# Ring order of layer one, a silu behind evictions, and the entrances of block 2's projections in halves

## What is computed

```python
def _layer(x, ctx, mod_lat, mod_ctx, ...):
    sh, sc, gt = jnp.split(mod_lat, 3, axis=-1)
    xn = _rms_norm(x, g_norm) * (1 + sc[:, None]) + sh[:, None]
    (au, av, az, bq, bk, bv, bz, cq, ck, cv, co, cz, cg) = _split_proj(xn @ w_in)
    ...
    y_a = _gmlp_branch(au, av, az, w_s, b_s)      # ... * silu(az)
    x = x + gt[:, None] * (jnp.concatenate([y_a, y_b, y_c], axis=-1) @ w_out)
...
def second_block(x, c, w_ada, ...):
    for i in range(DEPTH):
        mod = (ada_in @ w_ada[i] + b_ada[i]).reshape(b, 6, d)
        ...
        hm = rmsnorm(x, norm_mix[i]) * (1 + sc_m) + sh_m
        if i % N_MIXERS == 0:
            y = dilated_mixer(hm, ...)            # proj = hm @ w_in, 9216 columns
        else:
            y = forgetting_mixer(hm, ...)         # proj = hm @ w_in, 3088 columns
        x = x + g_m * y
        hf = rmsnorm(x, norm_ffn[i]) * (1 + sc_f) + sh_f
        x = x + g_f * hierarchical_moe(hf, ...)
```

## Time and profile before

| | us |
|---|---|
| median of 3 runs | 1784.41 |
| lowest, highest | 1781.46, 1784.58 |
| the profiled execution | 1783.85 |
| its span, first to last instruction | 1782.0 |
| PE busy | 1588.5 (89%) |
| DVE busy | 1001.6 (56%) |
| ACT busy | 680.4 (38%) |
| POOL busy | 168.3 (9%) |
| mean granted TensorE clock, share of 2.4 GHz | 0.902 |

### The profile page before, as it was taken

How to read it: one execution, slowest core, us unless ns; L and a number is a source line. 1 busy time by engine, 2 the same in 40 slices (tenths; PEclk the granted TensorE clock), 3 DMA queues, 4 the chain that set the end, 5 groups by cost and what they waited for, 6 DMA issues and landing times.

```text
span 1782.0 us, 19018 instructions
## 1 busy us (share of the span) xinstructions
PE 1588.5 (89%) x7325; PEld 1166.7 (65%) x7325; DVE 1001.6 (56%) x1573; ACT 680.4 (38%) x1081; POOL 168.3 (9%) x194
## 2 busy tenths in 40 slices
PE   5888986989899689799889999888999898979998
PEld 2757772564655455687777877647888676557886
DVE  2318436552466554576456754537777464257776
ACT  2311126311311331564115531125665566335663
POOL 1546620000000100200110001000000000000000
PEclk8999998769899878899789987889999898989999
DMA  8655511200465321767365744109888340049882
GB/s 308 247 165 177 176 48 41 80 1 19 170 236 199 131 95 49 216 214 254 93 160 177 257 164 121 58 2 316 299 303 283 120 163 27 1 157 315 296 294 95
DMA packets 186471, 290.70 MB, mean 163 GB/s; under 512 B 13739, under 2 KB 95115, under 8 KB 186380
## 3 DMA queue, kind: packets, MB, share of 16 engines
q1 hardware_dynamic: 171936, 272.93, 45.2%
q0 software_dynamic: 13200, 13.03, 3.4%
q10 hardware_dynamic: 1244, 3.52, 0.6%
HBM read 287.96 MB, written 1.49 MB: 162 GB/s over the span
## 4 chain that ended last, share of the span: by engine, by line
PE 71%; DVE 17%; ACT 6%; issue 2%; DMA 2%; SPq 2%; ACTq 0%; POOL 0%; DVEq 0%
PE ps L1098 31%; PE ps L2456 13%; PE ps L2366 3%; DVE P L1802 3%; PE ps L1279 2%; PE ps L1260 2%; ACT ps L1692 2%; DVE acc L1844 2%; PE ps L2474 2%; PE ps L2475 1%; PE ps L2476 1%; DVE E L1802 1%; PE ps L1268 1%; PE ps L1293 1%; DVE small L2036 1%
## 5 line engine op out<-in xcount | busy, mean ns | idle before, releaser
L1098 PE MATMUL ps<-WB,YP 128*128 128x512 f32 x1152 | 278.7, 401 | 13.6 <-DVE WB L1802 13.6
L1098 PEld LDWEIGHTS ps<-WB,YP 128*128 128x128 f32 x1152 | 219.2, 192 | 64.0 <-issue 12.9
L1802 DVE TENSOR_TENSOR WP<-ring,WP 128x2048 fp32r<-128x2048 f32 x96 | 218.9, 2290 | 50.1 <-ACT WP L678 49.8
L1098 PE MATMUL ps<-WP,XP 128*128 128x512 f32 x960 | 233.2, 396 | 9.5 <-DVE WP L1802 9.5
L1098 PEld LDWEIGHTS ps<-WP,XP 128*128 128x128 f32 x960 | 178.8, 189 | 47.3 <-DVE WP L1802 10.6
L678 ACT ACTIVATE WP<-ring 128x2048 fp32r<-128x2048 f32 x96 | 183.3, 1914 | 38.1 <-PE ps L1098 38.1
L1802 DVE TENSOR_TENSOR WB<-ring,WB 128x512 fp32r<-128x512 f32 x192 | 127.3, 690 | 92.0 <-ACT WB L608 90.3
L2456 PE MATMUL ps<-ring,XT 128*128 128x512 f32 (+3 forms) x448 | 169.8, 537 | 5.8 <-ACT XT L1628 3.3
L2456 PEld LDWEIGHTS ps<-ring,XT 128*128 128x128 f32 x448 | 89.0, 209 | 77.7 <-issue 65.8
L608 ACT ACTIVATE WB<-ring 128x512 fp32r<-128x512 f32 x192 | 113.1, 626 | 63.6 <-PE ps L1098 61.6
L1844 DVE SCALAR_TENSOR_TENSOR acc<-ring,silu_c,acc 128x512 f32<-128x512 f32 x168 | 126.1, 750 | 4.7
(11 more groups left out here) (346 smaller groups left out, 2264.1 us busy)
## 6 DMA issues: line engine op xcount, KB each, us to landing
ring<-in_w_ada SPq DMA_DIRECT2D x72, 1024.0 KB, 7.2
ring<-in_a_w_in SPq DMA_DIRECT2D x36, 1024.0 KB, 5.2
ring<-in_w_gate SPq DMA_DIRECT2D x64, 512.0 KB, 4.7
ring<-in_w_up SPq DMA_DIRECT2D x64, 512.0 KB, 5.8
ring<-in_w_down SPq DMA_DIRECT2D x32, 1024.0 KB, 6.9
ring<-in_w_in SPq DMA_DIRECT2D x24, 1024.0 KB, 7.3
ring<-in_b_w_in SPq DMA_DIRECT2D x12, 1024.0 KB, 5.3
ring<-in_w_out SPq DMA_DIRECT2D x8, 1024.0 KB, 5.1
```

The costliest lines, as they stand in the source:

```text
L1098: ins = mm(dst, x(a), w(b), start=(start and n == 0), stop=(stop_ and n == 2))
L1802: return v.tensor_tensor(out_, a, b, op)
```

## The change

1. **Ring order in layer one.** The first half of chunk n+1 is put before the modulation chunks that stand behind chunk n, its second half after them. The rows stay before items 10 and 22. No load is added or removed.
2. **The silu of AZ** moves from behind chunk 2 to behind chunk 3, before the GELU, on ACT and on VectorE, in both layers of block 1.
3. **Entrances.** `split_x` takes a half, and the first four weight blocks are split in between (`entrance`): half 0 of `XR`, blocks 0 and 1, half 1, blocks 2 and 3. TensorE waits for `y_lo` before blocks 0 and 4 of the first chunk. Before the forget projection ACT does all this ahead of the gates' evictions. For dilated half 1 the first four blocks are split in steps 8 to 11 of the attention of half 0.
4. TensorE's wait for `mods_done` before the output projection of the dilated attention goes.

```diff
 def ring_items():
@@
-    for n, (lo, hi) in enumerate(CHUNKS):
-        chunk("win", 0, lo, hi)
+    chunk("win", 0, *CHUNKS[0])
+    for n in range(len(CHUNKS)):
+        if n + 1 < len(CHUNKS):
+            items.append(("win", 0, *CHUNKS[n + 1], 0))
         for kind, layer, c in MODS_BEHIND[0].get(n, ()):
             chunk(kind, layer, c * 512, c * 512 + 512)
+        if n + 1 < len(CHUNKS):
+            items.append(("win", 0, *CHUNKS[n + 1], 1))
@@ ACT, block 2
-            def split_x(n):
-                act.wait_ge(S("xt_act"), 4 * n)
-                act.wait_ge(S("xt_dve"), 4 * n)
-                s_.activation(YP[:, 0], XR, ACT.Copy).then_inc(S("y_hi"), 1)
+            def split_x(n, half):
+                act.wait_ge(S("xt_act"), 4 * n + 2 * half - 2)
+                act.wait_ge(S("xt_dve"), 4 * n + 2 * half - 2)
+                ks = slice(4 * half, 4 * half + 4)
+                s_.activation(YP[:, 0, ks], XR[:, ks], ACT.Copy).then_inc(S("y_hi"), 1)
+            def high_of(item_kind, chunks, first, n, k):
...
+            def entrance(item_kind, chunks, first, x):
+                for half in range(2):
+                    split_x(x, half)
+                    for k in (2 * half, 2 * half + 1):
+                        high_of(item_kind, chunks, first, 0, k)
@@ ACT, qkv
                 act.wait_ge(S("pv"), c.at("units"))
-                for k in range(4):
-                    high(0, k)
@@ ACT, dilated_attention
-            def dilated_attention():
+            def dilated_attention(half):
                 c.up("row_max", 12)
                 for u in range(12):
                     s_.activation(PB2[:, u % 2], exponentials(u, 384), ACT.Exp).then_inc(S("probs"), 1)
+                    if half == 0 and u >= 8:
+                        high_of("awin", dilated_chunks(1), 9, 0, u - 8)
@@ ACT, order of the stages
-            split_x(3)
             act.wait_ge(S("gains"), 1)
+            entrance("awin", dilated_chunks(0), 0, 3)
...
-            split_x(5)
+            act.wait_ge(S("pv"), c.at("units"))
+            entrance("bwin", forget_chunks(), 18, 5)
             for t in range(2):
                 evict(FL[:, 16 * t:16 * t + 16], lambda b: b[:, 0:16])
@@ VectorE: split_x, low_of and entrance in the same manner; dilated_attention
                     if g == 0 and p > 0:
                         finals(4 * half + p - 1, bank(4 + (p - 1) % 2))
+                    if half == 0 and u >= 8:
+                        low_of("awin", dilated_chunks(1), 9, 0, u - 8)
                     c.up("pv")
                     next(ops, None)
@@ TensorE, qkv
                         q = 8 * (first + n) + k
+                        if n == 0 and k % 4 == 0:
+                            pe.wait_ge(S("y_lo"), 2 * x + k // 4 - 1)
                         pe.wait_ge(S("b_lo"), q + 1)
@@ TensorE, order of the stages
             norm_by_tile(LAT)
-            pe.wait_ge(S("y_lo"), 1)
             for half in range(2):
-                qkv("awin", dilated_chunks(half), 9 * half, True)
+                qkv("awin", dilated_chunks(half), 9 * half, 1, True)
                 dilated_attention(half)
-            pe.wait_ge(S("mods_done"), 4)
             out_part("awout", M2[:, 0, 16:24])
...
-            pe.wait_ge(S("y_lo"), 2)
-            qkv("bwin", forget_chunks(), 18, beside={1: sums_of_log_sigmoid})
+            qkv("bwin", forget_chunks(), 18, 2, beside={1: sums_of_log_sigmoid})
@@ post, on ACT and on VectorE
                 elif ci == 2:
                     rstd_small(hr, hs, HD)
+                elif ci == 3:
                     silu_part(AZ, AZ + 256, L, Ef)
-                elif ci == 3:
                     for t in range(0, len(L), 2):
                         gelu_part(L[t:t + 2])
```

More of the change, by code:

```diff
@@ L722, in act_block2 @@
             transposed_rows(LAT, lambda s: A2[:, 0, 0, :], lambda s: M2[:, 0, 0:8], dst=XR)
-            split_x(3)
             act.wait_ge(S("gains"), 1)
+            entrance("awin", dilated_chunks(0), 0, 3)
             for half in range(2):
                 qkv("awin", dilated_chunks(half), 9 * half, 0)
-                dilated_attention()
+                dilated_attention(half)
             gate_rows_out(1)
@@ L746, in dve_block2, with split_x, low_of, entrance @@
         def dve_block2(dve, c, invert_rstd, link, to, tt, ts, from_act, from_pe, ada_ops, ada_cols, pending, mods, norm, row_max, split_max, columns_of, out_proj, v):
-            def split_x(n):
-                dve.wait_ge(S("y_hi"), n)
-                tt(YP[:, 1], XR, YP[:, 0].bitcast(F32), ALU.subtract).then_inc(S("y_lo"), 1)
+            def split_x(n, half):
+                dve.wait_ge(S("y_hi"), 2 * n + half - 1)
+                ks = slice(4 * half, 4 * half + 4)
+                tt(YP[:, 1, ks], XR[:, ks], YP[:, 0, ks].bitcast(F32), ALU.subtract).then_inc(S("y_lo"), 1)
+            def low_of(item_kind, chunks, first, n, k):
+                if n == len(chunks):
+                    return
+                q = 8 * (first + n) + k
+                w, _ = block_weights(item_kind, 0, chunks, k, n)
+                b = block_slot(q)
+                dve.wait_ge(S("b_hi"), q + 1)
+                tt(b[:, 1], w, b[:, 0].bitcast(F32), ALU.subtract).then_inc(S("b_lo"), 1)
+            def entrance(item_kind, chunks, first, x):
+                for half in range(2):
+                    split_x(x, half)
+                    for k in (2 * half, 2 * half + 1):
+                        low_of(item_kind, chunks, first, 0, k)
             def qkv(item_kind, chunks, first, mod=None, beside={}):
@@ L757, in low @@
                 def low(n, k):
[L758 to L762, removed]
-                    dve.wait_ge(S("b_hi"), q + 1)
-                    tt(b[:, 1], w, b[:, 0].bitcast(F32), ALU.subtract).then_inc(S("b_lo"), 1)
+                    low_of(item_kind, chunks, first, n, k)
                     next(ops, None)
-                for k in range(4):
-                    low(0, k)
                 before = None
@@ L1099, in passes, with qkv @@
                 return ins
-            def qkv(item_kind, chunks, first, mod=False, beside={}):
+            def qkv(item_kind, chunks, first, x, mod=False, beside={}):
                 before = None
```

25 lines of the change are left out of this document (13 added, 12 removed).

## The result

The changed kernel took 1758.56 us in the median of its runs (1756.43 to 1766.49), the kernel before 1783.62 beside it: a ratio of 0.987 (95%: 0.984 to 0.990), 25.1 us less where 15.7 were forecast. The execution that was profiled took 1766.49 us, 17.4 less than the profiled one of before: in that pair the sum of steps is nearly right. The 7 to 10 us between this profile and the other runs are the first thing to explain, for they are not in the sum at all.

A forecast was written before the change was run, and what follows sets the result against it. TensorE was taken as the bound (71% of the chain), so only its idle time and the lower clock behind it could go. 12.0 + 2.2 + 1.6 - 0.7 + 0.6 = 15.7 us off 1784.41 gave 1769 us, range 1763 to 1777.5.

The forecast's parts named there:

- the sum of steps: Whole kernel: the gains and losses forecast for ring order, silu, entrances and dropped wait, added up to 15.7 us saved.
- Part 1, the ring: Layer one's projections: new ring order removes TensorE's waits before the last blocks of chunks 0 and 2, 13.9 us together.
- C: Layer one: first halves of chunks 2 and 6 land 8 us after issue, two stalls; gain 8.9, 1775.5 us; chance 0.05.
- E: Layer one: first halves land 14 us after issue, two stalls of 7.75 us each, kernel 3.6 us slower; chance 0.02.
- F: Layer one: a load before item 20 waits for a late slot, chunk 2's gap stays; gain 5.6, 1779 us; chance 0.04.
- The late rows: Layer one: row loads on SP's queue before item 22, from 88.3 to 105 us; a microsecond lost falls into slack.
- Part 2, the silu: Layer one: the move shifts TensorE's wait from chunk 4 to chunk 5, saves nothing, costs 1.9 us; layer two: 0.
- rival A: Layer one: POOL's splits stretch VectorE's chain by 3.1 us (1772 us) or 5.1 us (1774 us); chance 0.14.
- The price of 1.9 for the clock: Layer one, chunk 5: lower clock behind the moved wait costs 1.9 us, between 0 and 3.5.
- Part 3: Entrances in halves: dilated half 0 saves 2.2 us, the forget projection 1.6, dilated half 1 loses 0.7.
- `mods_done` and the forget entrance: Wait before the dilated output projection dropped, -0.6 us; forget projection's split ahead of gate evictions, -1.6 (-0.8 to -2.5).

## Why the prediction was right in most of its steps and wrong in its time

**What bounds the kernel, and the step that failed.** The prediction says that the change can only remove "time in which TensorE stands idle, and time at the lower clock behind such idle time". It was right in the first half, TensorE's idle time, and the second half is **the step that failed**: the sum has nothing for the stages in which no idle time was removed, so it takes their time at the lower clock as fixed. That term was put at nothing without a reason. The runs showed in its place that the attention of half 0 takes 64.3 or 59.8 to 61.4 us and that of half 1 65.6 to 65.9 or 56.7 to 56.8, by where they start against the grid. The grid's own place differs between executions (its last line lies 0.3 to 3.3 us before the first matmul). The Trainium skill (TensorE: Matmul & The Clock Gate, Part 1) has it that the gate's timing is free-running and isn't reset when a kernel starts, which these traces bear out. A second thing failed with it, the spread: the prediction took 3.6 us as what can be told from no change, and 119 runs of the kernel before lie over 28 us.

**Part 1, the ring**: the waits went as told, and chunk 2 ended at 112.27 for 112.3. POOL did wait for a DMA three times, for the first halves of chunks 2, 4 and 6, which the prediction names as a sign of C, E and F:

```profile
82.71 0.61 POOL L1526 CAST WH<-ring 128x512 fp32r<-128x512 f32 x1 [3.31 <-DMA ring<-in_w_in]
137.68 0.61 POOL L1526 CAST WH<-ring 128x512 fp32r<-128x512 f32 x1 [3.00 <-DMA ring<-in_w_in]
197.83 0.61 POOL L1526 CAST WH<-ring 128x512 fp32r<-128x512 f32 x1 [3.46 <-DMA ring<-in_w_in]
```

None of these waits reached TensorE, so the three rivals fell, and the sign was too wide. That the ring alone brought 14.5 (+-5.8) for 13.9 is luck in part, since its profile shows 10.1 up to matmul 1000. **The late rows** were mis-sized: SP was at them from 88.8 to 109.0, where I had 105, and two landings came behind their need. In the one run without these two waits matmul 1000 came 0.8 us sooner.

**Part 2, the silu**: the mechanism held (the wait went from chunk 4 to chunk 5, VectorE's chain set the time). The end of layer one's projections came 10.7 us sooner, not 12.0; over all profiles it is 9.7 in the mean (217.7 to 223.0 us up to matmul 1000 in the twelve with the new ring order, 228.2 to 231.9 in the six without). The chain was 64.3 us for 62.7, half of the smaller figure of rival A (3.1), and 63.6 to 64.3 in all profiles with the new ring order but the last, whether the silu was moved or not. VectorE did the same 67 instructions in it in 58.0 us for 56.5, beside the same 16 splits of POOL, and stood idle 6.3 us in both: A's mechanism in half its size, where the prediction added nothing. The price of 1.9 for the clock was 2.2 in one pair of kernels and 0 in another; that the silu's move helps is shown nowhere.

**Part 3**: half 0's entrance was right at its place, 2.80 us shorter (2.2 taken, 2.8 the end that I named). Here the missing term sits: the entrance of half 0 (-2.2) and that of half 1 (+0.7) were added up as if the attention behind each stayed as it was. The attention of half 0 took 64.3 us in all seven profiles in which its projection started 1.30 to 1.43 us after a grid line, and 59.8 to 61.4 in the eleven with 1.79 to 2.31. Within these eleven the start of the projection doesn't tell 59.9 from 61.3 (1.88 gave 59.85, 1.87 gave 61.35); the start of the attention itself (matmul 3250) does: 0.39 to 0.53 us after a line gave 59.8 to 59.9, 0.59 and 0.70 gave 61.3, 1.16 and 1.33 gave 60.8 and 60.9, 2.92 to 3.08 gave 64.3. The splits of half 1 cost 0.2 us. With them its attention took 56.7 or 56.8 us where that of half 0 had taken 64.3 or 59.9, and 65.7 or 65.8 where it had taken 60.9 to 61.4; without them it took 65.6 to 65.9 (the three kernels with an added matmul aside). The sum has +0.7 us for half 1 and nothing for half 0's attention; the attention stages measured -2.9 to -4.4 in half 0 and 0 or -8.8 in half 1. With the stage behind each it is -1.1 or -4.1, and 0 or -7.3, in the three profiles of the whole change.

**`mods_done` and the forget entrance**: idle time fell by 0.69 and 1.70 as forecast (-0.6, -1.6), but little came of the first (277.9 us for 278.0 in the stage behind half 1's attention) and nothing of the second. From matmul 5700 to the end of the span it is 381.2 us for 381.0. In five of the six profiles with the old forget entrance the last matmul starts 2.60 to 2.72 us after a grid line, whatever went before (in the sixth, that with the added matmul of 384 columns, 0.92); in all twelve with the new one it starts within 0.15 us of a line. Against the grid the end has very few places, which agrees with a saving there coming out as a step of the clock; no run tests it.

**The size.** In the profiled pair the time is 17.4 us less for 15.7 forecast, from deviations of both signs; that it comes so near is luck. Over many runs the change brings 22.2 (+-6.4) on one chip and 17.9 (+-4.5) on another, 19.3 (+-3.7) together, not 25. The median of few runs took in more of the short kinds than is their share: beside it the kernel before had four runs between 1781.5 and 1784.6 and none below 1775, which 42 of the 119 later ones reached. So 5.8 of the 9.4 us over the forecast come from comparing four runs with four. What is left, 3.6 us, is no more than the interval (+-3.7); it agrees in size with the attention stages, but that it is there, and that it is only these, is not shown.

**Still open**: why layer one's mLSTM takes 28.7 to 30.6 us in 7 of the 18 profiles and 39.5 to 40.5 in the others. Its start after a grid line orders them only in part (short at 0.74 to 0.80, 1.56, 1.60 and 3.11; long from 0.25 to 0.65, 2.1 to 2.8 and at 3.07), and I tried nothing on it. It is as long in the kernel before, so it adds to the spread and not, by anything seen here, to the gain (short in 5 of the 12 profiles with the new ring order and in 2 of the 6 with the old).

**A better kernel** was looked for among these. The change without the silu's move (-18.7) is as good as the whole change (-17.9) and no better by these intervals. A kernel whose half 1 always starts 2.2 us after a grid line should gain most, but in the changed kernel the start came at 1.93 and at 2.20 us, 0.27 apart. A delay that brings the first to 2.20 brings the second to 2.47, and at 2.41 the attention took 61.25. This is worked out from the table and not tried.

## What to carry to other kernels

Cut two traces at the same matmuls and compare lengths and granted clock stage by stage, before any step of a sum is called right or wrong: a sum that fits the total can be two errors, and here differences of 9 and 11 us sat in stages that the diff doesn't touch. A stage whose row shows a granted clock of 0.5 with TensorE nearly always busy may have a second, shorter kind, as the mLSTM has (37.9 us busy of 40.5); give the range room for it on both sides, and for each such stage. Where a change is worth about 1%, three runs that agree are no measure of it: take the mean of a dozen, on one chip, and look at each run's clock.

## What the runs showed of the hardware that was not expected

- Work added can shorten: one matmul of 384 columns in front of a stage, and the stage took 56.7 us for 65.6.
- Work added can cost nearly 20 times itself: one matmul of 512 columns (0.23 us) in the changed kernel and the attention of half 1 took 61.25 us, where the profiles that start 2.20 to 2.26 us after a grid line have 56.8; two cost 8.2 us (+-4.6) in the mean of the runs.
- TensorE nearly always busy isn't TensorE at the upper clock: in the kernel before the mLSTM ran 40 us at a granted clock of 0.50 with 94% of the time busy, with matmuls of 65 to 128 columns.
- The start of a stage against the grid draws together along the kernel: at matmul 1000 it lies anywhere (0.02 to 3.36 us), at the start of half 0's projection between 1.3 and 2.3, and at the end at one of three places.
- Small loads on SP's queue have no fixed price: two row loads (of `w_s` and of the experts' router) took 3.48 and 3.49 us for the first layer and 2.15 and 0.58 for the second, in one stretch of 20 us.
